# Weighting expert outputs per slot, adding both results of a token by gather, and keeping expert weights in a decoder step on one core

## What is computed

```python
def hmoe(h, ...):
    # group top-1 -> expert top-2 of 16 experts; gates: one weight per (token, expert)
    for e in range(N_EXPERTS):
        a = jax.nn.silu(h @ w_eg[e]) * (h @ w_eu[e])          # 1024 -> 256
        out = out + gates[..., e:e + 1] * (a @ w_ed[e])       # 256 -> 1024
x  = x + g_a * (mix @ w_out)
h2 = modulate(rms_norm(x, norm2_g), sh_m, sc_m)
x  = x + g_m * hmoe(h2, ...)      # g_m: one row for the prompt, one for each sequence
y  = rms_norm(x, final_norm_g)
```

## Time and profile before

| | |
|---|---|
| median of 3 runs | 1577.04 us (1575.16 to 1581.68) |
| the profiled execution | 1575.7 us, of which the span is 1574.0 us |
| granted TensorE clock, mean over the span | 0.888 of full speed |
| busy: PE, DVE, ACT, POOL | 1327.0, 657.7, 375.6, 141.3 us |
| moved by DMA | 219.97 MB |

### The profile page before, as it was taken

How to read it: one execution, slowest core, us unless ns; L and a number is a source line. 1 busy time by engine, 2 the same in 40 slices (tenths; PEclk the granted TensorE clock), 3 DMA queues, 4 the chain that set the end, 5 groups by cost and what they waited for, 6 DMA issues and landing times.

```text
span 1574.0 us, 14505 instructions
## 1 busy us (share of the span) xinstructions
PE 1327.0 (84%) x4792; PEld 699.8 (44%) x4792; DVE 657.7 (42%) x1364; ACT 375.6 (24%) x786; POOL 141.3 (9%) x214
## 2 busy tenths in 40 slices
PE   5899989993089999788999999994999999999930
PEld 2775625341035565354444545554444444444410
DVE  2204479999923319953454413334011111111139
ACT  5214300310024410143555511110111111111124
POOL 0100210000000020222000000000111111111040
PEclk9899969996589968876999999985999999999975
DMA  9202670100030000336000011102989999998844
GB/s 358 74 1 107 220 278 0 53 0 0 0 80 1 1 4 27 109 106 173 1 1 1 28 40 54 70 31 68 374 330 338 335 337 326 339 331 331 305 186 171
DMA packets 78418, 219.97 MB, mean 140 GB/s; under 512 B 26343, under 2 KB 40871, under 8 KB 63001
## 3 DMA queue, kind: packets, MB, share of 16 engines
q1 hardware_dynamic: 61436, 163.76, 29.5%
q0 software_dynamic: 16928, 55.51, 9.7%
HBM read 191.14 MB, written 28.11 MB: 139 GB/s over the span
## 4 chain that ended last, share of the span: by engine, by line
PE 64%; DVE 17%; issue 11%; ACT 3%; DMA 2%; DVEq 0%; POOL 0%; SPq 0%; ACTq 0%; POOLq 0%
PE psum L1256 14%; PE psum L1195 8%; PE psum L877 8%; PE psum L1273 8%; PE psum L1127 5%; PE psum L1167 5%; DVE marks L1746 5%; PE psum L1158 2%; PE psum L900 2%; DMA mem<-in_w_ada 2%; PE psum L835 1%; DVE mem L1677 1%; PE psum L1265 1%; PE psum L1214 1%; PE psum L959 1%
## 5 line engine op out<-in xcount | busy, mean ns | idle before, releaser
L877 PE MATMUL psum<-mem 128*128 128x512 f32 (+5 forms) x576 | 180.0, 472 | 78.3 <-ACT mem L1356 72.8
L1256 PE MATMUL psum<-mem 128*128 128x512 f32 x512 | 227.2, 597 | 1.1 <-ACT mem L1584 1.1
L900 PE MATMUL psum<-mem 128*128 128x512 f32 (+1 forms) x480 | 167.1, 515 | 0.0
L877 PEld LDWEIGHTS psum<-mem 128*128 128x128 f32 (+1 forms) x576 | 95.9, 186 | 155.3 <-issue 75.8
L1256 PEld LDWEIGHTS psum<-mem 128*128 128x128 f32 x512 | 98.0, 192 | 124.8 <-issue 123.3
L1273 PE MATMUL psum<-mem 128*128 128x512 f32 x256 | 118.4, 605 | 15.2 <-ACT mem L1594 15.2
L1195 PE MATMUL psum<-mem 128*128 128x512 f32 (+1 forms) x288 | 124.9, 592 | 0.8 <-issue 0.8
L900 PEld LDWEIGHTS psum<-mem 128*128 128x128 f32 x480 | 87.0, 213 | 81.1 <-issue 81.1
L1746 DVE TENSOR_SCALAR_CACHE_REDUCE marks<-mem,top_try_low 128x384 uint16<-128x384 uint16 (+6 forms) x112 | 104.0, 993 | 0.6
L2085 DVE COPY mem<-psum 128x1024 f32<-128x1024 f32 x32 | 39.2, 1225 | 154.1 <-PE psum L1273 154.1
L2081 DVE TENSOR_TENSOR mem<-psum,mem 128x256 f32<-128x256 f32 x32 | 13.6, 425 | 212.9 <-ACT mem L1590 212.9
(11 more groups left out here) (338 smaller groups left out, 1485.4 us busy)
## 6 DMA issues: line engine op xcount, KB each, us to landing
mem<-in_w_exp_gate SPq DMA_DIRECT2D x32, 1024.0 KB, 6.6
mem<-in_w_exp_up SPq DMA_DIRECT2D x32, 1024.0 KB, 8.7
mem<-in_w_exp_down SPq DMA_DIRECT2D x32, 1024.0 KB, 8.3
mem<-in_w_ada SPq DMA_DIRECT2D x24, 1024.0 KB, 10.3
y_of_slot<-mem POOLq DMA_DIRECT2D x32, 512.0 KB, 7.7
mem<-in_x_prompt SPq DMA_DIRECT2D x16, 512.0 KB, 4.6
mem<-in_w_in SPq DMA_DIRECT2D x3, 2048.0 KB, 8.1
h_rows<-mem POOLq DMA_DIRECT2D x8, 512.0 KB, 2.9
```

The lines of the kernel that those rows point to most:

```text
L877: mm = pe.matmul(bank[0:rows(i), to:to + width], h_t[:, k, cols(i)], w[:, k, c0:c0 + width], start=(k == 0), stop=(k == KT - 1))
L900: mm = pe.matmul(bank[0:width, 0:n_t], w[:, k, c0:c0 + width], h_t[:, k, t0:t0 + n_t], start=(k == 0), stop=(k == KT - 1))
L1256: mm = pe.matmul(psum[:, 2 + u, :].rearrange("p (n f) -> p n f", n=2), x_slot_t[:, u, k, :], w_gu[u][:, :, k, :], start=(k == 0), stop=(k ...
```

## The change

- **Order on PE and ACT.** The loop of the experts is written out. The down product of block `j-1` now stands between the transposes of block `j+1`'s activations and those of block `j`'s hidden values. ACT copies the next activations ahead of the turned hidden values.
- **Weights.** Three slots. Expert `e` lies in slot `e % 3`, and its weights are loaded for the first of its blocks alone: the three DMAs of a block carry a condition. PE reads the slot's offset of each block from `w_at_i` into a register, and SP reads three numbers per block. Every expert gets at least one block, so block 0 is expert 0's and is loaded before the routing is known.
- **Weight and gate per slot.** Two more one-hot products of 18 each bring the routing weight (`weight_of`) and the sequence number (`seq_i`) of each slot. POOL gathers a gate row for each slot. DVE multiplies by both while it takes the result out of PSUM.
- **Tail.** The gathers of both results add into `x1` as they land, nine for the first results and then nine for the second, each of these behind the first one's landing. The scaling on ACT and three operations per tile on DVE are gone.
- **Queues.** The near key pages are loaded as soon as the projections before them are done, ahead of the wait for the selection, on SP and on POOL. The five row loads of `gate_m` on POOL are gone.
- Six semaphores of the linear attention's gates are merged into two counters, with the same waits; small buffers lie elsewhere.

```diff
+W_SLOTS, W_SLOT = 3, 6144
-        "full_before": np.broadcast_to(P * np.arange(TILES)[None, :], (P, TILES)),
+        "full_before": np.broadcast_to((P * np.arange(TILES) - (np.arange(TILES) == 0))[None, :], (P, TILES)),
...
+            sp.wait_ge(s_proj, first_dq)
+            for b in range(RING - 1):
+                load_pages(nc.sync, b, found, "cache_k", near_pages, s_kp)
             sp.wait_ge(s_top, TOP_STEPS)
             for b in range(RING, NSEQ - 1):
                 load_pages(nc.sync, b, found, "cache_k", far_pages, s_far)
-            sp.wait_ge(s_proj, first_dq)
-            for b in range(RING - 1):
-                load_pages(nc.sync, b, found, "cache_k", near_pages, s_kp)
...
+            load_gate_up(0, 0, 0, {})
+            load_down(0, 0, 0, {})
+            sp.wait_ge(s_experts_known, 1)
+            for j in range(1, BLOCKS):
+                e = sp.value_load(expert_i[0:1, j:j + 1], min_val=0, max_val=NE - 1)
+                to = sp.value_load(w_at_i[0:1, j:j + 1], min_val=0, max_val=W_SLOT * (W_SLOTS - 1))
+                is_new = sp.value_load(is_new_i[0:1, j:j + 1], min_val=0, max_val=1)
+                if j >= W_SLOTS:
+                    sp.wait_ge(s_gate_up, j - W_SLOTS + 1)
+                load_gate_up(j, e, to, {"cond": is_new})
+                if j >= W_SLOTS:
+                    sp.wait_ge(s_down, j - W_SLOTS + 1)
+                load_down(j, e, to, {"cond": is_new})
...
+            pool.wait_ge(s_ids_known, 2)
+            gather_gates(0)
+            gather_gates(1)
+            for j in range(BLOCKS + GATHERED_BEFORE):
+                if j + GATHERED_BEFORE < BLOCKS:
+                    pool.wait_ge(s_x_slot_turned, j + 1)
+                    gather_x(j + GATHERED_BEFORE)
+                if j >= GATHERED_BEFORE:
+                    stored = j - GATHERED_BEFORE
+                    pool.wait_ge(s_y_rows, stored + 1)
+                    pool.dma_start(y_of_slot[stored * P:(stored + 1) * P, :], y_rows[:, stored % 2, :]).then_inc(s_ys[stored % 2], 16)
+                    if stored + 2 < BLOCKS:
+                        gather_gates(stored + 2)
...
+                pool.indirect_dma_start(x1[0:r, i, :], None, y_of_slot, bass.IndirectOffsetOnAxis(at_pair, axis=0),
+                                        compute_op=ALU.add).then_inc(s_yp[(i + 1) // 2], 16)
+            for i in range(TILES):
+                add_to_x1(i, 0)
+            for i in range(TILES):
+                if i == 0 or i % 2 == 1:
+                    pool.wait_ge(s_yp[(i + 1) // 2], 32 if i else 16)
+                add_to_x1(i, 1)
...
             mm.then_inc(s_ids_turned, 1)
+            pe.wait_ge(s_slots_marked, 2)
+            for of_slot, to in ((slot_weight, 3), (slot_seq, 4)):
+                for m in range(2 * TILES):
+                    mm = pe.matmul(psum[:, to, 0:BLOCKS], slot_low[:, m, :], of_slot[:, m, :], start=(m == 0), stop=(m == 2 * TILES - 1))
+            mm.then_inc(s_ids_turned, 1)
...
+            pe.wait_ge(s_experts_known, 1)
+            w_at = [0] * BLOCKS
+            for j in range(BLOCKS):
+                w_at[j] = weights_of(j)
+                gate_up(j, w_at[j])
+                if j + 1 < BLOCKS:
+                    turn_x(j + 1, (j + 1) % 2, (j + 1) // 2)
+                if j >= 1:
+                    down(j - 1, w_at[j - 1])
+                turn_hid(j)
+            down(BLOCKS - 1, w_at[BLOCKS - 1])
...
-                act.activation(y_a[0:r, i, :], y_a[0:r, i, :], copy, scale=w_pair[0:r, 0, i:i + 1]).then_inc(s_y_weighed, 1)
...
+            step(dve.tensor_tensor(slot_weight, slot_block, over(w_pair.rearrange("p n i -> p (n i)"), 2 * TILES, BLOCKS), ALU.mult))
+            step(dve.tensor_tensor(per_pair(slot_seq), per_pair(slot_block), of_token("seq_no"), ALU.mult))
+            dve.tensor_tensor(per_pair(slot_block), per_pair(slot_block), of_token("token_no"), ALU.mult).then_inc(s_slots_marked, 2)
...
-                dve.tensor_copy(y_rows[:, u, :].rearrange("p (c d) -> p c d", c=2), psum[:, 6:8, :]).then_inc(s_y_rows, 1)
+                dve.wait_ge(s_ids_known, 2)
+                dve.wait_ge(s_gates[u], 16 * (j // 2 + 1))
+                dve.scalar_tensor_tensor(y_rows[:, u, :].rearrange("p (c d) -> p c d", c=2), psum[:, 6:8, :], weight_of[:, j:j + 1],
+                                         gate_rows[:, u, :].rearrange("p (c d) -> p c d", c=2), ALU.mult, ALU.mult).then_inc(s_y_rows, 1)
...
-                n = own.did(dve.scalar_tensor_tensor(y, y_b[0:r, i, :], w_pair[0:r, 1, i:i + 1], y, ALU.mult, ALU.add))
-                n = own.did(dve.tensor_tensor(y, y, gate_m[0:r, g, :], ALU.mult))
-                dve.tensor_tensor(x1[0:r, i, :], x1[0:r, i, :], y, ALU.add).then_inc(s_y_sum, 1)
```

More of the change, by code:

```diff
@@ L730, in _ @@
             pool.sem_inc(s_pool_prepared, 1)
[L733 removed]
+            pool.wait_ge(s_gate_dve, GQ_READY)
             for j in range(2):
@@ L1266, in expert_block, with down @@
                 t.then_inc(s_hid_turned, 1)
+            def down(j, w_at):
+                u, w_dn = j % 2, down_at(w_at)
                 pe.wait_ge(s_hid_t, j + 1)
-                pe.wait_ge(s_ed[u], 16 * (occurrence + 1))
-                if not (first and u == 0):
+                pe.wait_ge(s_ed[j % W_SLOTS], 16 * (j // W_SLOTS + 1))
+                if j >= 1:
                     pe.wait_ge(s_y_rows, j)
@@ L1413, in _ @@
             own.wait(n)
-            act.activation(tmp_t, tmp_t, ACT.Ln, bias=K("one")).then_inc(s_softplus, 1)
+            act.activation(tmp_t, tmp_t, ACT.Ln, bias=K("one")).then_inc(s_gate_act, 1)
             KEPT_LATER = 3
@@ L1613, in final_norm @@
                 act.activation(y_rstd[0:r, i:i + 1], y_ss[0:r, i:i + 1], ACT.Sqrt, scale=1.0 / D, bias=K("eps", r)).then_inc(s_y_rstd, 1)
-            for i in range(TILES):
-                r = rows(i)
-                act.wait_ge(s_yp[(i + 1) // 2], 64 if i else 32)
-                act.activation(y_a[0:r, i, :], y_a[0:r, i, :], copy, scale=w_pair[0:r, 0, i:i + 1]).then_inc(s_y_weighed, 1)
-                if i >= 1:
-                    final_norm(i - 1)
-            final_norm(TILES - 1)
         @block.vector
@@ L2073, in _ @@
             step(dve.tensor_reduce(expert_f, ended, AX.X, ALU.add))
-            dve.tensor_scalar(expert_i[:, :], expert_f[0:1, :], float(NE - 1), None, ALU.min).then_inc(s_experts_known, 1)
-            def expert_block(j, u, occurrence, first):
+            step(dve.tensor_scalar(expert_f, expert_f, float(NE - 1), None, ALU.min))
+            own.did(dve.tensor_copy(expert_i[:, :], expert_f[0:1, :]))
+            own.did(dve.memset(is_new_i[:, 0:1], 0))
+            own.did(dve.tensor_tensor(is_new_i[:, 1:], expert_f[0:1, 1:], expert_f[0:1, 0:BLOCKS - 1], ALU.subtract))
@@ L2078, in expert_block @@
+            for j in range(BLOCKS):
+                u = j % 2
                 dve.wait_ge(s_silu_g, j + 1)
-                if not first:
+                if j >= 2:
                     dve.wait_ge(s_hid_turned, j - 1)
                 dve.tensor_tensor(hid[:, u, :], psum[:, 2 + u, DE:2 * DE], silu_g[:, u, :], ALU.mult).then_inc(s_hid, 1)
-                dve.wait_ge(s_down, j + 1)
-                if not first:
-                    dve.wait_ge(s_ys[u], 16 * occurrence)
-                dve.tensor_copy(y_rows[:, u, :].rearrange("p (c d) -> p c d", c=2), psum[:, 6:8, :]).then_inc(s_y_rows, 1)
@@ L2087, in _ @@
-            for u in range(2):
-                expert_block(u, u, 0, True)
-            with dve.Fori(1, BLOCKS // 2) as jj:
-                for u in range(2):
-                    expert_block(2 * jj + u, u, jj, False)
-            dve.wait_ge(s_tailw, 16 * 6)
-            def add_pair(i):
-                r, g = rows(i), int(i == NT)
-                dve.wait_ge(s_yp[(i + 1) // 2], 64 if i else 32)
-                dve.wait_ge(s_y_weighed, i + 1)
-                y = y_a[0:r, i, :]
-                n = own.did(dve.scalar_tensor_tensor(y, y_b[0:r, i, :], w_pair[0:r, 1, i:i + 1], y, ALU.mult, ALU.add))
-                own.wait(n)
-                n = own.did(dve.tensor_tensor(y, y, gate_m[0:r, g, :], ALU.mult))
-                own.wait(n)
-                dve.tensor_tensor(x1[0:r, i, :], x1[0:r, i, :], y, ALU.add).then_inc(s_y_sum, 1)
```

209 lines of the change are left out of this document (99 added, 110 removed).

## The result

| | before | after |
|---|---|---|
| median | 1576.85 us (4 runs, 1575.16 to 1581.68) | 1555.43 us (4 runs, 1554.42 to 1556.43) |
| profiled execution, span | 1575.7, 1574.0 us | 1554.9, 1553.0 us |
| granted TensorE clock | 0.888 | 0.886 |
| moved by DMA | 219.97 MB | 185.97 MB |

The account below looks back on a forecast made before the run. It saw a chain of stages with no single leading line, PE's short waits in the experts and DVE setting the tail's end. Terms -23.5 + 12.6 + 0 + 0.7 = -10.2 us gave 1567; range 1541 to 1586, forecast's own 1558 to 1575.

Parts of the forecast that it names:

- Order on PE, -23.5 us: Experts: both short waits of PE go, beat from 12.56 to 11.80 us over 31 steps; ends 18.6 and 29.8.
- a free addition: Rival, tail: an adding gather costs no more than a copy, 22.7 us more gained, 1544; chance 0.20.
- the clock that rises (1559): Rival, ahead of the experts: clock rises in the narrow products, 7.9 us more gained, 1559; chance 0.04.
- PE's register load, 0: Experts: PE's register load per block is hidden behind 3.5 us of queued down product, so costs nothing.
- Weights kept, 0: Experts: 16 loads of 3 MB fall away, but DMA was never waited for, so no time is gained.
- The DMA share of 0.6: Experts: sign expected in the profile after, a DMA share near 0.6.
- Ahead of the experts, +12.6: Before the first gate product: two DVE operations add 1.6 us, added PE products 11.0 at the cold clock.
- Tail, 0: After the last down product: gathers that add set the end, 1574.4 against 1574.0, so nothing gained.
- the doubled price: Tail: an adding gather costs twice a copy, 2.65 us per full tile; the price the forecast took.
- the single price: Tail: an adding gather costs the same as a copy, 1.32 us; end at 1551.3, so -22.7 us.
- Key pages, +0.7: Key selection: early loads are hidden anyway, but PE idles longer before the masks and starts cold, losing 0.7 us.
- the one in which the beat isn't shortened: Rival, experts: something else, such as DMA, holds the beat at 12.56 us: +13.3, 1590; chance 0.03.

Follow-up runs that it names:

- e1: Changed kernel with the old order of PE, ACT and DVE in the experts put back: 1590.19 us, ratio 1.0088 against the kernel before.
- e4: Changed kernel with three register loads on PE per block in place of one: 1555.05 us, ratio 0.9862 against the kernel before.
- e3: Changed kernel with all weights loaded for every block, no condition and no register load on PE: 1553.49 us, ratio 0.9862 against the kernel before.
- e2: Kernel before with only the new order of PE, ACT, DVE and POOL in the experts, loops written out: 1577.81 us, ratio 1.002.
- e10: e2 with SP issuing the next block's gate and up weights before its wait for the down product: 1543.81 us, ratio 0.9801 against the kernel before.
- e6: Changed kernel with one one-hot product of 96 columns in place of three of 32: 1541.68 us, ratio 0.9785 against the kernel before.
- e5: Changed kernel with the addition left out of the tail's 18 gathers, so sums are missing: 1532.61 us, ratio 0.9729 against the kernel before.
- e9: Changed kernel with the edits of e6 and e7 together: 1529.88 us, ratio 0.9698 against the kernel before.
- e12: e9 with one semaphore per tile, gathers adding only tile 7's second result and both of the 32-row tile: 1525.85 us, ratio 0.9684 against the kernel before.
- e7: Changed kernel with plain gathers of both results and both additions on DVE: 1542.49 us, ratio 0.979 against the kernel before.

## Why the prediction was right and wrong

*Order on PE, -23.5 us: the step that failed, a mis-sized term.* The mechanism was right: both waits went, nothing on ACT or DVE took their place, and e1 gives all of it back. The term, priced by a beat of 11.80 us, measured 31 x (12.56 - 11.42) = 35.3 us, and 33.9 over the stage (the first gate product was 0.6 us longer, and the wait of 1.3 us at the end is new), outside its own ends of 18.6 and 29.8. The prediction took 0.60 us of idle time off and then kept the busy times of the earlier trace rows nearly whole, with 11.60 as the lowest end. In the closed stream (no wait within a block) the work is, from start to start, 6.87 + 0.89 + 3.44 + 0.22 = 11.42 us: 0.16 off the eight transposes, 0.29 off the two, 0.10 off the down product. I read these as drains: beside a wait the time in which the pipeline runs empty counts in full, in the stream the next records start within it. The starts show the sizes; the reason is argued.

So the miss of 0.38 us a block has two halves. The prediction's own terms add up to 11.61 (0.25 off the two transposes, 0.10 off the down product), and it then took 11.80, halfway back to 11.96, for which no row speaks: 0.19. And it had seen that the two transposes hold a drain, but priced them by the eight (0.26 in place of 0.22) and kept the eight whole, which held one themselves: 0.04 and 0.16. With 11.42 the term would have been 35 and the sum -22. That the time still lies in the range is owed to the range, which was made wide for a free addition; the rival nearest in time, the clock that rises (1559), did not happen.

*PE's register load, 0:* right (e4). *Weights kept, 0:* right (e3). The argument missed one thing: what the order does to SP's queue. With the queue of before it cost the whole gain (e2). Three slots hide it, for then the down product that SP waits for lies a block further back, and e3 shows PE fed in full that way; they are not needed for it (e10). The DMA share of 0.6 that I had named was 0.83 at 310 GB/s.

*Ahead of the experts, +12.6:* 12.05 within the stage, and 12.3 counted from the start of the span, the key pages' part regained by then. PE stayed at 0.50, which is 1.2 GHz, through 22.9 us of products of 32 columns without a gap, so the rival in which the clock rises fell. The rule of "TensorE: Matmul & The Clock Gate", section "Why this matters for your kernels" of the Trainium skill, that keeping TensorE continuously busy brings the full clock, did not come true there; in e6, with 96 columns, it did. The 40 us at 0.50 of the earlier trace rows were read a little too simply: they end with three records of 512 columns, and as these products go on the clock is 0.76 from 600 to 602 and 1.00 from 602 to 604. Up to 596 the widest product had 128 columns, so the price taken from them stands.

*Tail, 0:* right, 0.6 us. From the first gather to the end 59.6 us passed, and the doubled price had given 59.1. e5 gives the other end: 38.3 us, where the single price had given 36.0. The half rate that "Collectives: The Full Stack", section "The bandwidth ceiling: the fold count and why AG ≠ RS ≠ AR", of the Trainium skill states for an add in collectives fits these gathers: 200 to 211 GB/s against 396 in the earlier trace rows.

*Key pages, +0.7:* 0.55 at the product behind the masks, 0.1 by 1045, nothing in the sum. (It was eight semaphores, not six, that were merged; of that, too, nothing shows by 1045.) Of the rivals not named so far, the one in which the beat isn't shortened fell too.

## What to carry to other kernels

Before pricing the closing of a gap, take the work from start-to-start times in a stretch without waits: busy times beside a wait came out 0.55 us too long here, in a beat of 12.56. Between two ends that rows give, don't take the middle without a row. When an order on one engine is changed, walk every queue that waits for it: a load behind a wait that moved a block later cost 34 us in e2, and putting the loads ahead of that wait gave it back. Of a change of many parts, run the main part alone: here it was faster than the whole (e10). An addition in a gather is paid by the DMA engines at the price of a second transfer; where they are full and DVE could add, two plain gathers and DVE are faster (12.9 us here), and a table of three in one product costs less than three products (13.7 us).

## What had not been expected of the hardware

- Float32 products of 32 columns held PE busy for 22.9 us and the clock stayed at 0.50, in the change and in every kernel here that keeps its three products. The same 18 pairs with 96 columns saw it rise from 0.50 to 1.00, but not always alike: in e6 and e9, where they start at 1092.6 and 1092.5, it is 1.00 from 1096.6 on; in e12, where they start at 1093.4, it is still 0.50 up to 1100. Two shapes are seen here, no threshold, and what sets the moment stays open.
- DMA moved 414 GB/s beside products at full clock (e3, and 425 for 4 us in the kernel before), where a share of 0.91 at 337 in the earlier trace rows had seemed to promise 370: GB/s by share is no measure of the ceiling.
- POOL's issue of a gather that adds took 1.55 us in the mean, of one that copies 0.99 (e5). Whether that is the work of the issue or a full queue behind it stays open. It costs nothing here: the issues come 1.87 us apart, and 0.52 MB at 205 GB/s keep the DMA engines busy for 2.6.
- An operation of DVE on 32 rows of 1024 took 1.20 us, on 128 rows 1.22 (e7): the short ninth tile costs a full one.
